# Sliding attention taken in visits of four steps instead of two, its turned weights kept in six places, two of the projection's PSUM banks given up to it

## The chip, the cores and the metric

One NeuronCore of one Trainium2 chip runs the whole program in one launch. The metric is the device time of that launch in microseconds (us), lower is better. TensorE is called PE below (PEld is its weight load), VectorE DVE, ScalarE ACT, GpSimd POOL, and SyncE SP; SP only issues DMAs.

## The reference, cut to what matters

The program computes two transformer blocks and a final norm over 512 tokens of width 1024. Only one part of the second block is touched: its input projection, the sliding-window attention that is computed while that projection runs, and the first product behind them.

```python
z = h @ w_in + b_in                     # 512 x 1024 @ 1024 x 5376 -> 42 tiles of 128 columns
glu_val, glu_gate, q, k, v, g_conv, g_attn = split(z)
q, k = rope(q), rope(k)                 # 16 query heads, 2 key/value heads, head size 64
# blocks of 128 queries see their own and the previous block of 128 keys
s = where(mask, einsum(q, k) * 64 ** -0.5, -1e30)
m = maximum(max(s), sink)
p = exp(s - m) / (sum(exp(s - m)) + exp(sink - m))
attn_out = (p @ v) @ w_attn_o           # 512 x 1024 @ 1024 x 1024
conv_out = conformer_conv(glu_val, glu_gate, ...)   # 31 taps over time, then a layer norm, then a product
```

## The kernel before, in words

Everything is written out by hand: each engine has one instruction stream, and semaphores (`wait_ge`, `then_inc`) tie them together. An engine does its instructions strictly in that order, so one wait holds up all that stands behind it.

**Big products.** Each float32 matrix is split into a high part (rounded, `wh`, `hh`) and a low part (what the rounding left, `wl`, `hl`). `three` (L1383, L1384, L1385) adds three matmuls of 128x128 by 128x512 into a PSUM bank. Eight such triples (index `k`) make one output tile; one triple is called a chunk below. Weights come in slots of 1 MB, each good for two tiles. A slot goes through four hands: SP loads it to `raw[:, b, :]` (`load`, L493, or `load_raw_after`, L550), ACT rounds it to `wh` (`high`, L736), DVE subtracts to get `wl` (`weight_low`, L2059, which raises `w_lo`), and PE uses it. `b` is the slot's number modulo 2, so there are two places for each. Eight slots of the projection (`SPLIT0` and on) were split earlier and come ready from DRAM into `w2` without passing through `raw`; the last slot of the projection (number 69, tiles 40 and 41) and the slots of the next product, "ao", (numbers 70 to 73) go through `raw` again. Slot 70 is the first block of ao, and uses `raw[:, 0, :]`.

**The projection, "in2".** 42 tiles, numbered `t`. Each is written to the bank `IN2_BANKS[t]`; three banks are used in turn from tile 6 on. ACT empties the bank (`in2_out`, L1145, raises `ev_in2`), and PE waits for `ev_in2` of tile `t - 3` before it begins tile `t`.

**Sliding attention.** 32 steps: 8 pairs of heads (`p`) by 4 blocks of queries (`i`). Both heads of a pair are done in one step (`e`). The first block of a pair has 128 key columns, the others 256. A step `n` goes through

- `scores` (PE, L1716): queries times keys, into banks 3 and 4, a half bank for each of two steps
- `masked` (DVE, L2461): scaling, mask and maximum, into `spr[:, n % 2]`
- `exps` and `scaled` (ACT, L1093 to L1105): the softmax
- `turn` (PE, L1727): the weights are transposed into bank 5
- `turned_weights` (ACT, L1114): bank 5 is copied to `spt[:, n % 2]`, in `sqb`
- `values` (PE, L1740): the values times these, into bank 6 or 7
- `heads_out` (ACT, L1121 and L1127), once in four steps, and `y_low` (DVE, L2469, raises `at_l`): the pair's result, split in high and low part for ao.

The steps are spread over tiles 22 to 41 in 35 **beats**. `beat_place` puts beat `n` before chunk `n * 160 // 35` of these tiles, so one comes after every four or five chunks. At a beat PE leaves the projection, does its attention work (a **visit**), and goes back. At an even beat `n` the visit holds `scores` of steps `n` and `n + 1`, `values` of steps `n - 4` and `n - 3`, and `turn` of step `n - 2`; at an odd beat only the `turn`. DVE and ACT have beats of their own in the same order. Between them DVE does the 31 taps of the convolution (`taps`, L2400), 256 instructions of about the same size that fill its time.

**Behind the projection.** ao begins when `w_lo` says that slot 70 is complete. Its first tile takes in piece `k` only when `at_l` has reached `k + 1`, so its last piece waits for `y_low(7)`. ao's fourth and sixth tiles hold the two means of the layer norm (`mean_of_parts`, L1390), for which DVE must have finished the taps and the sums.

## Time and profile before

| | us |
|---|---|
| median of 3 runs (2585.38 to 2585.94) | 2585.47 |
| profiled execution, its own time | 2584.94 |
| its span in the trace | 2583.1 |
| PE busy in the span | 2571.9 |
| DVE, ACT, POOL busy | 1638.5, 1061.1, 426.9 |
| stage of the beats (first `scores` to the last `values`) | 731.3 to 884.6 |

The trace counts from the start of the span. PE's busy time is the union of its matmuls, whose ends are modelled, so a busy PE can still be held back by what stands between two matmuls; the distance from the start of one matmul to the start of the next shows it. In steady work of the projection that distance is 0.227 us.

### The profile page before, as it was taken

The page shows a single profiled execution, that of the slowest core. Times are in us where ns is not written, and L with a number is a line of the kernel's source. Part 1 is how long each engine was busy: PE and PEld are TensorE (multiplying, and loading weights), DVE is VectorE, ACT ScalarE, POOL GpSimd, SP SyncE. Part 2 cuts the span into 40 slices and gives each one's busy share as a digit, 9 for nine tenths or more (in the row PEclk, how much of TensorE's full clock was granted, in tenths as well). Part 3 has the DMA queues.
Part 4 walks back from the last instruction along what each step waited for, and adds up shares of the span by engine and source line. Part 5 has one row for each costly group of instructions (what it writes and reads, how often), then busy time and mean ns, then how long its engine had stood idle before and what let it go on. Part 6 is the DMA issues. An engine that isn't in the chain of part 4 may idle for free.

```text
span 2583.1 us, 33615 instructions
## 1 busy us (share of the span) xinstructions
PE 2571.9 (100%) x12592; PEld 2114.2 (82%) x12592; DVE 1638.5 (63%) x2450; ACT 1061.1 (41%) x1408; POOL 426.9 (17%) x188
## 2 busy tenths in 40 slices
PE   9999999999999999999999999999999999999999
PEld 7778888888877788888888888888888888888887
DVE  6777322304999986689997999999244444444444
ACT  6765433215367753232223555555322222222223
POOL 0002555542022014434443000000000000000000
PEclk9999999999999999999999999999999999999999
DMA  5112664222234222323333455655676655555553
GB/s 190 66 50 82 260 244 179 102 98 98 102 115 163 98 96 100 114 90 146 146 146 147 173 189 191 241 204 187 244 224 207 201 192 191 191 192 190 191 190 126
DMA packets 143324, 410.58 MB, mean 159 GB/s; under 512 B 25552, under 2 KB 91344, under 8 KB 111376
## 3 DMA queue, kind: packets, MB, share of 16 engines
q1 hardware_dynamic: 138400, 353.53, 39.8%
q10 hardware_dynamic: 2016, 34.87, 3.4%
q0 software_dynamic: 2832, 21.24, 2.4%
q8 instruction: 39, 0.64, 0.1%
q14 instruction: 37, 0.30, 0.0%
HBM read 319.16 MB, written 85.98 MB: 157 GB/s over the span
## 4 chain that ended last, share of the span: by engine, by line
PE 98%; ACT 1%; DVE 1%; issue 0%; DMA 0%; SPq 0%; ACTq 0%; DVEq 0%
PE ps L1383 31%; PE ps L1385 30%; PE ps L1384 30%; PE ps L1962 2%; PE ps L1912 1%; PE ps L1716 1%; PE ps L1727 1%; PE ps L1740 1%; PE ps L1598 0%; PE ps L1625 0%; PE ps L1609 0%; DMA raw<-in_w_slots 0%; DVE z L2400 0%; ACT w L736 0%; PE ps L1528 0%
## 5 line engine op out<-in xcount | busy, mean ns | idle before, releaser
L1383 PE MATMUL ps<-hh,w 128*128 128x512 f32 x1968 | 775.3, 394 | 2.3 <-DVE w L2065 2.3
L1385 PE MATMUL ps<-hh,w 128*128 128x512 f32 x1968 | 766.9, 390 | 0.0
L1384 PE MATMUL ps<-hl,w 128*128 128x512 f32 x1968 | 765.8, 389 | 0.0
L736 ACT ACTIVATE w<-raw 128x2048 fp32r<-128x2048 f32 x207 | 395.7, 1912 | 739.9 <-PE ps L1385 739.8
L2694 DVE TENSOR_TENSOR w<-raw,w 128x2048 fp32r<-128x2048 f32 x101 | 231.3, 2290 | 419.4 <-ACT w L736 419.4
L1383 PEld LDWEIGHTS ps<-hh,w 128*128 128x128 f32 x1968 | 369.5, 188 | 86.5 <-issue 7.4
L1385 PEld LDWEIGHTS ps<-hh,w 128*128 128x128 f32 x1968 | 369.4, 188 | 78.4
L1384 PEld LDWEIGHTS ps<-hl,w 128*128 128x128 f32 x1968 | 369.8, 188 | 74.1
L1383 PE MATMUL ps<-w,gah 128*128 128x512 f32 x1024 | 398.3, 389 | 0.0
L1384 PE MATMUL ps<-w,gah 128*128 128x512 f32 x1024 | 398.3, 389 | 0.0
L1385 PE MATMUL ps<-w,gal 128*128 128x512 f32 x1024 | 398.3, 389 | 0.0
L635 POOL TENSOR_TENSOR w<-raw,w 128x2048 fp32r<-128x2048 f32 x50 | 230.5, 4611 | 567.1 <-ACT w L736 567.1
L1385 PEld LDWEIGHTS ps<-w,gal 128*128 128x128 f32 x1024 | 192.3, 188 | 39.9
L1384 PEld LDWEIGHTS ps<-w,gah 128*128 128x128 f32 x1024 | 192.3, 188 | 39.9
L1383 PEld LDWEIGHTS ps<-w,gah 128*128 128x128 f32 x1024 | 192.3, 188 | 39.8
L723 POOL TENSOR_TENSOR pf<-xT,final_rows 128x512 f32<-128x512 f32 x4 | 5.2, 1300 | 1171.0 <-DVE xT L2769 1171.0
L2400 DVE SCALAR_TENSOR_TENSOR z<-z,vec 128x511 f32<-128x511 f32 (+14 forms) x240 | 160.4, 730 | 0.0
L715 POOL TENSOR_TENSOR w<-raw,w 128x2048 fp32r<-128x2048 f32 x27 | 127.1, 4706 | 182.1 <-ACT w L736 182.1
L1272 ACT ACTIVATE ast<-ps 128x512 f32<-128x512 f32 x64 | 38.2, 599 | 239.2 <-PE ps L1385 239.2
L1317 ACT ACTIVATE stage<-ps 128x512 f32<-128x512 f32 x128 | 124.0, 1133 | 0.0
L1307 ACT ACTIVATE ast<-ps 128x512 f32<-128x512 f32 x64 | 38.3, 598 | 194.3 <-PE ps L1385 194.3
L2708 DVE TENSOR_TENSOR same<-iota_t,slot_t 128x1024 f16<-128x1024 f16 x64 | 78.5, 1226 | 43.3 <-PE ps L1962 33.3
(320 smaller groups left out, 3092.6 us busy)
## 6 DMA issues: line engine op xcount, KB each, us to landing
raw<-in_w_slots SPq DMA_DIRECT2D x208, 1024.0 KB, 4.8
a_spill<-ast SPq DMA_DIRECT2D x64, 512.0 KB, 4.7
gate_table<-stage ACTq DMA_DIRECT2D x8, 4096.0 KB, 12.1
at<-a_spill SPq DMA_DIRECT2D x64, 512.0 KB, 5.9
tt<-gate_table SPq DMA_DIRECT2D x64, 512.0 KB, 7.0
w<-split_weights POOLq DMA_DIRECT2D x8, 2048.0 KB, 8.2
split_raw<-in_w_slots SPq DMA_DIRECT2D x8, 1024.0 KB, 6.8
split_weights<-hidl SPq DMA_DIRECT2D x8, 1024.0 KB, 3.8
```

What stands on the lines that cost most here:

```text
L635: pool.tensor_tensor(wl[:, b, :], raw[:, b, :], wh[:, b, :].bitcast(F32), ALU.subtract).then_inc(sem("w_lo"), 1)
L715: pool.tensor_tensor(wl[:, b, :], raw[:, b, :], wh[:, b, :].bitcast(F32), ALU.subtract).then_inc(sem("uv_lo"), 1)
L736: act.activation(wh[:, b, :], raw[:, b, :], ACT.Copy).then_inc(sem("w_hi"), 1)
L1307: act.activation(ast[:, 2 * (i % 2) + j, :], ps[:, 4 + 2 * (i % 2) + j, :], ACT.Gelu).then_inc(sem("a_ev"), 1)
L1317: act.activation(stage[:, q % 2, :, c:c + 4].rearrange("p e c -> p c e"), ps[:, 2 * j + a, :].rearrange("p (c e) -> p c e", c=4), ACT.Copy ...
L1383: nc.tensor.matmul(bank, whi, xhi, start=start, stop=False, skip_group_check=reopened)
L1384: nc.tensor.matmul(bank, whi, xlo, start=False, stop=False, skip_group_check=reopened)
L1385: return nc.tensor.matmul(bank, wlo, xhi, start=False, stop=stop, skip_group_check=reopened)
L1962: last = nc.tensor.matmul(ps[:, 2 * r + t // 4, NKEYS * (t % 4):NKEYS * (t % 4) + NKEYS], oh[r][:, 0, t, :], oh[r][:, part, t, :], start=( ...
L2400: dve.scalar_tensor_tensor(acc[:, back:S], u[:, 0:S - back], w, acc[:, back:S], ALU.mult, ALU.add).then_inc(sem("cv2_y" if m == TAPS else ...
L2694: dve.tensor_tensor(wl[:, b, :], raw[:, b, :], wh[:, b, :].bitcast(F32), ALU.subtract).then_inc(sem("uv_lo"), 1)
L2708: dve.tensor_tensor(same[:, :, :], iota_rows, slots(0), ALU.is_equal).then_inc(sem("oh_part"), 1)
```

## The change

1. PE's visits: `scores` and `values` are done for four steps at once, every fourth beat. `scores` of steps `n` to `n + 3` at beats 0, 4, ..., 28; `values` of steps `n - 8` to `n - 5` at beats 8, 12, ..., 32, and of the last four steps at beat 34. `turn` stays at each beat.
2. The scores need four half-bank pairs: banks 3 and 4, and banks 1 and 7. Bank 1 is taken from the projection, whose tiles from 21 on use banks 0 and 2 in turn, and PE waits for `ev_in2` of tile `t - 2`. `values` uses bank 6, and for the last pair bank 7.
3. The turned weights have six places: two in `sqb`, four in `raw[:, 0, :]`, which is idle while slots come ready from DRAM.
4. Therefore SP loads slot 70 only when `values` of all 32 steps is done (`sw_o`). ACT's `high` for it moves from tile 39 to tile 40 of its order; DVE's `weight_low` stays at tile 40, with five taps put before it.
5. ACT empties a tile's bank before the beats of the next tile instead of behind them; `heads_out` and `y_low` come two beats later; ao's first tiles wait for other semaphores, as their banks are other ones.

```diff
+TWO_BANKS = BEAT_TILE0 - 1
+IN2_BANKS = [1, 2, 0, 3, 4, 5] + [(t + 1) % 3 for t in range(6, TWO_BANKS)] + [t % 2 * 2 for t in range(TWO_BANKS, Z2_TILES)]
+SCORE_BANKS = ((3, 4), (1, 7))
+VALUE_BANKS = [6] * (SWA_PAIRS - 1) + [7]
+TURNED_SLOTS = 6
...
+        def spt(n):
+            r = n % TURNED_SLOTS
+            rows = sqb[:, r, :] if r < 2 else raw[:, 0, (r - 2) * S:(r - 1) * S]
+            return rows.rearrange("p (e n) -> p e n", e=2)
...
             for g in (after, after + 1):
                 sp.wait_ge(sem("w_used"), g - 1)
+                if g % 2 == 0:
+                    sp.wait_ge(sem("sw_o"), SWA_STEPS)
                 load_raw_after(g)
...
                 act.wait_ge(sem("sw_t"), n + 1)
-                if n >= 2:
-                    act.wait_ge(sem("sw_o"), n - 1)
+                if n == 0:
+                    act.wait_ge(sem("w_lo"), SPLIT0 + 2)
+                if n >= TURNED_SLOTS:
+                    act.wait_ge(sem("sw_o"), n - TURNED_SLOTS + 1)
...
-                if n >= 7 and (n - 7) % NT == 0:
-                    heads_out((n - 7) // NT)
+                if n >= 9 and (n - 9) % NT == 0:
+                    heads_out((n - 9) // NT)
...
             for t in range(Z2_TILES + 1):
+                if t > TWO_BANKS:
+                    in2_out(t - 1)
                 for n in beats_in(t):
                     beat(n)
...
-                if t >= 4:
+                if 4 <= t <= TWO_BANKS:
                     in2_out(t - 1)
...
+                late = t in (Z2_TILES - 3, Z2_TILES - 2)
+                if late and t % 2 == 0:
+                    high(g0 + t // 2 + 1, (g0 + t // 2 + 1) % 2)
...
-                if n % 2 == 0:
+                if i == 0:
                     pe.wait_ge(sem("sw_q"), p + 1)
-                    if n:
-                        pe.wait_ge(sem("sw_m"), 2 * n)
+                if n % 2 == 0 and n >= NT:
+                    pe.wait_ge(sem("sw_m"), 2 * n - NT)
...
             def beat(n):
-                if n % 2 == 0:
-                    for m in (n, n + 1):
-                        if m < SWA_STEPS:
-                            scores(m)
-                    for m in (n - 4, n - 3):
-                        if 0 <= m < SWA_STEPS:
-                            values(m)
+                if n % NT == 0 and n < SWA_STEPS:
+                    for m in range(n, n + NT):
+                        scores(m)
+                if n % NT == 0 and n >= 2 * NT:
+                    for m in range(n - 2 * NT, n - NT):
+                        values(m)
+                if n == BEATS - 1:
+                    for m in range(SWA_STEPS - NT, SWA_STEPS):
+                        values(m)
                 if 0 <= n - 2 < SWA_STEPS:
                     turn(n - 2)
...
-                    pe.wait_ge(sem("ev_in2"), t - 2)
+                    pe.wait_ge(sem("ev_in2"), t - 2 if t < TWO_BANKS else t - 1)
...
-                if n < 3:
-                    pe.wait_ge(sem("ev_in2"), Z2_TILES - 2 + n)
+                if n in (1, 2):
+                    pe.wait_ge(sem("ev_in2"), Z2_TILES)
                 elif n < 5:
                     pe.wait_ge(sem("sw_m"), 2 * SWA_STEPS)
...
-                if n >= 9 and (n - 9) % NT == 0:
-                    y_low((n - 9) // NT)
+                if n >= 11 and (n - 11) % NT == 0:
+                    y_low((n - 11) // NT)
...
                         dve.sem_inc(sem("w_lo"), SPLIT_SLOTS)
+                    if t == Z2_TILES - 2:
+                        taps(5)
                     weight_low(g0 + t // 2 + 1)
...
-            taps(12)
+            y_low(SWA_PAIRS - 2)
+            taps(7)
             y_low(SWA_PAIRS - 1)
             weight_low(g0 + 1)
             taps(KD * conv_steps)
```

How the change moves instructions, at three places. First PE at beat 8, where a pair of heads begins (`scores` write `ps` from `kdup`, `values` read `sqb` or `raw`, `turn` reads `tmp_all`). Before, the whole visit:

```order
L1716 MATMUL ps<-kdup,z 128x128 [waits sw_m,sw_q]
L1716 MATMUL ps<-kdup,z 128x128
L1716 MATMUL ps<-kdup,z 128x256 x2
L1740 MATMUL ps<-sqb,z 64x128 [waits sw_pt]
L1740 MATMUL ps<-sqb,z 64x128
L1740 MATMUL ps<-sqb,z 64x128 [waits sw_pt]
L1740 MATMUL ps<-sqb,z 64x128 x3
L1727 MATMUL ps<-cst,tmp_all 128x128 [waits sw_pt,sw_p]
L1727 MATMUL ps<-cst,tmp_all 128x128 x3
```

and with the change, from the third step's `scores` on (the first two stand ahead of it as before):

```order
L1735 MATMUL ps<-kdup,z 128x256 [waits sw_m]
L1735 MATMUL ps<-kdup,z 128x256 x3
L1761 MATMUL ps<-sqb,z 64x128 [waits sw_pt]
L1761 MATMUL ps<-sqb,z 64x128
L1761 MATMUL ps<-sqb,z 64x128 [waits sw_pt]
L1761 MATMUL ps<-sqb,z 64x128 x3
L1761 MATMUL ps<-raw,z 64x128 [waits sw_pt]
L1761 MATMUL ps<-raw,z 64x128 x3
L1761 MATMUL ps<-raw,z 64x128 [waits sw_pt]
L1761 MATMUL ps<-raw,z 64x128 x3
L1746 MATMUL ps<-cst,tmp_all 128x128 [waits sw_pt,sw_p]
```

Four steps' `scores` and `values` stand where two were; beats 6 and 10 keep only their `turn`.

Second ACT at the end of the projection, around `turned_weights` of steps 30 and 31 (L1114; L1145 is `in2_out`, L736 `high`, L1121 and L1127 `heads_out`). Before:

```order
L1145 ACTIVATE z<-ps,vec 128x512 [waits half_mm]
L736 ACTIVATE w<-raw 128x2048 [waits w_used,w_raw0]
L1114 ACTIVATE sqb<-ps 128x512 [waits sw_o,sw_t] x2
L1145 ACTIVATE z<-ps,vec 128x512 [waits w_used]
L1145 ACTIVATE z<-ps,vec 128x512 [waits half_mm]
L736 ACTIVATE w<-raw 128x2048 [waits w_used,w_raw1]
L1145 ACTIVATE z<-ps,vec 128x512 [waits w_used]
L1121 ACTIVATE z<-ps 128x512 [waits sw_o]
L1127 ACTIVATE csinr<-z 128x512 [waits sw_q,sw_y]
```

and with the change (the same helpers are L1128, L1159, L748, L1135 and L1141):

```order
L1128 ACTIVATE sqb<-ps 128x512 [waits sw_o,sw_t] x2
L1135 ACTIVATE z<-ps 128x512 [waits sw_o]
L1141 ACTIVATE csinr<-z 128x512 [waits sw_q,sw_y]
L748 ACTIVATE w<-raw 128x2048 [waits w_used,w_raw0]
L1159 ACTIVATE z<-ps,vec 128x512 [waits half_mm]
L748 ACTIVATE w<-raw 128x2048 [waits w_used,w_raw1]
L1159 ACTIVATE z<-ps,vec 128x512 [waits w_used]
L1135 ACTIVATE z<-ps 128x512 [waits sw_o]
L1141 ACTIVATE csinr<-z 128x512 [waits sw_q,sw_y]
```

`high` of slot 70 (`w_raw0`) stood before `turned_weights` of steps 30 and 31, and now stands behind them and behind a `heads_out`.

Third DVE, behind `weight_low` of slot 70, from the last of three taps to `weight_low` of slot 71, with the change (L2423 is one tap, L2492 `y_low`, L2082 `weight_low`):

```order
L2423 SCALAR_TENSOR_TENSOR z<-z,vec 128x490 [waits cv2_1]
L2492 TENSOR_TENSOR z2r<-z,csinr 128x512 [waits at_h]
L2423 SCALAR_TENSOR_TENSOR z<-z,vec 128x489 [waits cv2_0]
L2423 SCALAR_TENSOR_TENSOR z<-z,vec 128x489 [waits cv2_1]
L2423 SCALAR_TENSOR_TENSOR z<-z,vec 128x488 [waits cv2_0]
L2423 SCALAR_TENSOR_TENSOR z<-z,vec 128x488 [waits cv2_1]
L2423 SCALAR_TENSOR_TENSOR z<-z,vec 128x487 [waits cv2_0]
L2423 SCALAR_TENSOR_TENSOR z<-z,vec 128x487 [waits cv2_1]
L2423 SCALAR_TENSOR_TENSOR z<-z,vec 128x486 [waits cv2_0]
L2492 TENSOR_TENSOR z2r<-z,csinr 128x512 [waits at_h]
L2082 TENSOR_TENSOR w<-raw,w 128x2048 [waits w_hi]
```

Before, both low parts stood apart by fifteen taps and one `y_low`; with the change it is ten taps and two `y_low`, and five taps have gone ahead of slot 70's.

## Rows read from the trace of the kernel before

**Rows 1.** Page of the profile: busy time, share of the span, instructions.

```profile
PE 2571.9 (100%) x12592; PEld 2114.2 (82%) x12592; DVE 1638.5 (63%) x2450; ACT 1061.1 (41%) x1408; POOL 426.9 (17%) x188
```

**Rows 2.** Waits of 731 to 884 us: total, times, longest.

```profile
DVE tmp_all L2461 <- PE ps L1727: 10.4, 11, 1.6
...
PE ps L1727 <- ACT sqb L1114: 0.6, 1, 0.6
```

**Rows 3.** Timeline of PE, visits of beats 4 and 6: start, length, merged.

```profile
746.58 0.93 PE L1716 MATMUL ps<-kdup,z 64*128 64x128 f32 x8
747.44 0.93 PE L1740 MATMUL ps<-sqb,z 128*64 128x128 f32 x12
748.29 0.66 PE L1727 MATMUL ps<-cst,tmp_all 128*128 128x128 f32 x4
...
755.18 0.39 PE L1385 MATMUL ps<-hh,w 128*128 128x512 f32 x1
755.50 1.13 PE L1716 MATMUL ps<-kdup,z 64*128 64x256 f32 x8
756.57 1.15 PE L1740 MATMUL ps<-sqb,z 128*64 128x128 f32 x16
757.64 0.44 PE L1727 MATMUL ps<-cst,tmp_all 128*128 128x128 f32 x2
...
758.15 0.39 PE L1384 MATMUL ps<-hl,w 128*128 128x512 f32 x1
```

**Rows 4.** Timeline of PE, visit of beat 3, a turn alone.

```profile
742.37 0.40 PE L1385 MATMUL ps<-hh,w 128*128 128x512 f32 x1
742.60 0.60 PE L1727 MATMUL ps<-cst,tmp_all 128*128 128x128 f32 x4
...
743.28 0.39 PE L1384 MATMUL ps<-hl,w 128*128 128x512 f32 x1
```

**Rows 5.** Timeline of PE, turns of beats 29 and 33.

```profile
860.96 0.39 PE L1385 MATMUL ps<-hh,w 128*128 128x512 f32 x1
861.47 0.63 PE L1727 MATMUL ps<-cst,tmp_all 128*128 128x128 f32 x4
...
878.48 0.39 PE L1385 MATMUL ps<-hh,w 128*128 128x512 f32 x1
879.46 0.63 PE L1727 MATMUL ps<-cst,tmp_all 128*128 128x128 f32 x4 [0.59 <-ACT sqb L1114]
```

**Rows 6.** Timeline of PE: last values, first ao matmul, ao's eighth piece.

```profile
883.45 1.15 PE L1740 MATMUL ps<-sqb,z 128*64 128x128 f32 x16
...
888.06 0.39 PE L1383 MATMUL ps<-z2r,w 128*128 128x512 f32 x1
...
892.82 0.42 PE L1383 MATMUL ps<-csinr,w 128*128 128x512 f32 x1
```

**Rows 7.** Timeline of ACT: high part of slot 70.

```profile
876.93 1.90 ACT L736 ACTIVATE w<-raw 128x2048 fp32r<-128x2048 f32 x1
```

**Rows 8.** Timeline of DVE: fifteen taps, last y_low, low part of slot 71.

```profile
881.30 9.68 DVE L2400 SCALAR_TENSOR_TENSOR z<-z,vec 128x493 f32<-128x493 f32 x15
891.99 0.69 DVE L2469 TENSOR_TENSOR z2r<-z,csinr 128x512 fp32r<-128x512 f32 x1 [1.01 <-ACT csinr L1127]
892.60 2.29 DVE L2059 TENSOR_TENSOR w<-raw,w 128x2048 fp32r<-128x2048 f32 x1
```

**Rows 9.** Source L550: the two loads behind the ready slots.

```profile
DMA to landing us min/median/max: 4.7/4.8/4.8
```

**Rows 10.** Timeline of DVE, then PE: layer norm's second mean.

```profile
920.38 0.69 DVE L2045 TENSOR_TENSOR sqr<-z,sqr 128x512 fp32r<-128x512 f32 x1
...
921.26 0.39 PE L1390 MATMUL ps<-sqr,cst_r 128*128 128x512 f32 x1
```

**Rows 11.** Stretches at the end: PE, PEld, DVE, ACT, POOL; PEclk, DMA, GB/s.

```profile
2576.00:2578.00 2.00, 1.18 (x6) 0.64 (x4) 1.33 (x4) 1.87 (x6) 1.29 (x1) 1.00 0.41 153
...
2579.00:2580.00 1.00, 0.00 (x0) 0.00 (x0) 0.74 (x1) 0.81 (x2) 0.00 (x0) 0.62 0.42 160
```

More of the change, by code:

```diff
@@ L213 @@
 RAW_TILES = 6
-IN2_BANKS = [1, 2, 0, 3, 4, 5] + [(t + 1) % 3 for t in range(6, Z2_TILES)]
+TWO_BANKS = BEAT_TILE0 - 1
[3 more added lines that the diff above has]
+TURNED_SLOTS = 6
 def rolled(eng, n, unroll, body):
@@ L1111, in turned_weights @@
                 act.wait_ge(sem("sw_t"), n + 1)
[L1112 to L1114 removed]
+                if n == 0:
+                    act.wait_ge(sem("w_lo"), SPLIT0 + 2)
+                if n >= TURNED_SLOTS:
+                    act.wait_ge(sem("sw_o"), n - TURNED_SLOTS + 1)
+                act.activation(spt(n).rearrange("p e (b n) -> p e b n", b=2)[:, :, b:, :],
                                ps[:, 5, :].rearrange("p (e b n) -> p e b n", e=2, b=2)[:, :, b:, :], ACT.Copy
@@ L1120, in heads_out @@
                 act.wait_ge(sem("sw_o"), NT * p + NT)
-                act.activation(u_tile(Q2 + p), ps[:, 6 + p % 2, :], ACT.Copy).then_inc(sem("sw_y"), 1)
+                act.activation(u_tile(Q2 + p), ps[:, VALUE_BANKS[p], :], ACT.Copy).then_inc(sem("sw_y"), 1)
                 act.wait_ge(sem("sw_y"), p + 1)
@@ L1174, in _ @@
                         in2_out(a)
-                if t < Z2_TILES and t % 2 and t != RAW_TILES - 1 and not is_split(g0 + t // 2 + 2):
+                late = t in (Z2_TILES - 3, Z2_TILES - 2)
+                if late and t % 2 == 0:
+                    high(g0 + t // 2 + 1, (g0 + t // 2 + 1) % 2)
+                if t < Z2_TILES and t % 2 and not late and t != RAW_TILES - 1 and not is_split(g0 + t // 2 + 2):
                     if g0 + t // 2 + 2 == SPLIT0 + SPLIT_SLOTS:
@@ L1709, in scores @@
                 kv, r = p // PAIRS_PER_KV, n % 2 * 2 * P
-                if n % 2 == 0:
+                if i == 0:
                     pe.wait_ge(sem("sw_q"), p + 1)
-                    if n:
-                        pe.wait_ge(sem("sw_m"), 2 * n)
+                if n % 2 == 0 and n >= NT:
+                    pe.wait_ge(sem("sw_m"), 2 * n - NT)
                 for e in range(2):
                     h = slice(HD * e, HD * e + HD)
-                    last = nc.tensor.matmul(ps[:, 3 + e, r + c:r + 2 * P], z2[h, Q2 + p, i * P:i * P + P],
+                    last = nc.tensor.matmul(ps[:, SCORE_BANKS[n // 2 % 2][e], r + c:r + 2 * P], z2[h, Q2 + p, i * P:i * P + P],
                                             kdup[h, kv, (i - 1) * P + c:(i + 1) * P], start=True, stop=True)
@@ L1735, in values @@
                 pe.wait_ge(sem("sw_pt"), n + 1)
-                if i == 0 and p > 1:
-                    pe.wait_ge(sem("sw_y"), p - 1)
+                if i == 0 and p == SWA_PAIRS - 1:
+                    pe.wait_ge(sem("sw_m"), 2 * SWA_STEPS)
+                elif i == 0 and p:
+                    pe.wait_ge(sem("sw_y"), p)
                 for e in range(2):
                     for k in range(c, 2 * P, P):
-                        last = nc.tensor.matmul(ps[HD * e:HD * e + HD, 6 + p % 2, i * P:i * P + P],
+                        last = nc.tensor.matmul(ps[HD * e:HD * e + HD, VALUE_BANKS[p], i * P:i * P + P],
                                                 vn(i - 1 + k // P)[:, HD * kv:HD * kv + HD],
-                                                spt[:, n % 2, e, k:k + P], start=(k == c), stop=(k == P))
+                                                spt(n)[:, e, k:k + P], start=(k == c), stop=(k == P))
                 last.then_inc(sem("sw_o"), 1)
             def beat(n):
-                if n % 2 == 0:
-                    for m in (n, n + 1):
-                        if m < SWA_STEPS:
-                            scores(m)
-                    for m in (n - 4, n - 3):
-                        if 0 <= m < SWA_STEPS:
-                            values(m)
+                if n % NT == 0 and n < SWA_STEPS:
[7 more added lines that the diff above has]
+                        values(m)
                 if 0 <= n - 2 < SWA_STEPS:
@@ L2460, in masked @@
                 for e in range(2):
-                    dve.tensor_tensor_reduce(spr[:, n % 2, e, c:2 * P], ps[:, 3 + e, r + c:r + 2 * P], msk[:, c:], -SCALE,
+                    dve.tensor_tensor_reduce(spr[:, n % 2, e, c:2 * P], ps[:, SCORE_BANKS[n // 2 % 2][e], r + c:r + 2 * P], msk[:, c:], -SCALE,
                                              nsink[:, 2 * p + e:2 * p + e + 1], ALU.add, ALU.min,
```

2 lines of the change are left out of this document (removed).

## The prediction

> **What bounds the kernel now.** I read the page first. PE is busy for 2571.9 us of a span of 2583.1 [rows 1], so the other engines matter only where PE waits for them, and every hundredth of a microsecond between two of its matmuls counts. Next I asked for the waits of the stage that the change touches, 731 to 884 us. PE hardly waits there: 0.6 us in all is booked, on `turned_weights`. DVE on the other hand waits 10.4 us for PE's turns [rows 2], so it has that much to spare in the stage. What PE loses there is not waiting but switching, and that is seen only in the starts of its matmuls, so the third view was PE's timeline.
>
> A steady product of the projection starts 0.227 us after the one before it. The seven pieces between ao's first matmul and its eighth piece (21 matmuls) take 892.82 - 888.06 = 4.76 us, which is 0.227 each and 0.68 for a chunk [rows 6]. A visit is what its neighbours are apart beyond that. A turn alone costs 743.28 - 742.37 - 2 x 0.227 = 0.46 us for its four matmuls, 0.114 each [rows 4]. The visit of beat 6 costs 758.15 - 755.18 - 2 x 0.227 = 2.52 us [rows 3].
>
> How much of the 2.52 is work? I compare it with beat 4, which has the same groups with less in them [rows 3].
> - `scores` to `values`: 1.07 us for eight matmuls of 256 columns, 0.86 where four of the eight have 128. Halving four saves 0.21, so four of 256 are 0.42 and eight 0.84. Left: 0.23 for the switch.
> - `values` to `turn`: 1.07 us for sixteen matmuls, 0.85 for twelve. Four are 0.22, sixteen 0.88. Left: 0.19.
> - Entry: 755.50 - 755.18 - 0.227 = 0.09 us.
> - Two turns and the way back: 758.15 - 0.227 - 757.64 = 0.28 us against 0.23 at the price of rows 4. Left: 0.05.
>
> So a visit with both `scores` and `values` costs 0.56 us over its work, and a turn alone nothing.
>
> **The change, part by part.**
>
> *Fewer visits.* Before, `scores` and `values` meet at beats 4, 6, ..., 30: 14 visits. With the change they meet at 8, 12, ..., 28: six. The visits with only one of them are two and two in both. All matmuls stay. Saved: 8 x 0.56 = **4.5 us**.
>
> *Late turns.* At beats 29 and 33 the turn starts 861.47 - 860.96 = 0.51 and 879.46 - 878.48 = 0.98 us after the product before it [rows 5], 0.28 and 0.75 more than the steady 0.227. Both follow a `high` on ACT, 1.90 us long [rows 7], which stands before the `turned_weights` that the turn needs. The change puts the second `high` behind both copies, and a `heads_out` no longer stands before the first. Saved: **1.0 us**.
>
> *New waits in the stage.* None of them is in the trace, so I bound them. (a) The third `scores` of a visit waits for `masked` of the step before the visit. DVE has 10.4 us to spare over the stage [rows 2], and PE becomes at most 5.5 us faster, so on the whole DVE keeps up; but the visits at which only a turn is left come about 2 us sooner after the last one. (b) With two banks PE needs tile `t - 2` emptied; ACT does that before the next beats. (c) ACT's copies have up to 2 us less before a turn at every second even beat. The least is nothing. For the most I take that half of each of the seven later `scores` visits waits as long as the first late turn, 0.28 us, and that two tiles and two turns wait as much: 7.5 x 0.28 = 2.1 us. I take 0.5, near the lower end, because of the 10.4 us.
>
> Together PE comes to the end of `values` 4.5 + 1.0 - 0.5 = **5.0 us** earlier.
>
> *The load of slot 70.* Here the time is given back. Before, the last `values` ends at 883.45 + 1.15 = 884.60 [rows 6]; now at 879.6. Only then may SP issue the load. Five chunks of the projection are left to PE, and before it went over to ao without a gap at 888.06 [rows 6]; now it would at 883.1. But the load lands after 4.8 us [rows 9], at 884.4; ACT rounds for 1.90 [rows 7], to 886.3; DVE subtracts for 2.29 [rows 8], to **888.6**. PE stands idle for 5.5 us, and ao begins 0.5 us later than before. The next load, of slot 71, is issued right behind, and PE needs it only at ao's third tile, 10.9 us later: covered.
>
> *What stands behind the low part on DVE.* DVE comes to `weight_low` of slot 70 long before 886.3: between `masked(31)` and it there are 14 taps of 9.68 / 15 = 0.645 us and one `y_low` [rows 8]. So it waits too, and the order holds everything else up. Behind it come three taps, `y_low(6)`, seven taps and `y_low(7)`: 10 x 0.645 + 2 x 0.61 = 7.7 us (0.61 is 892.60 - 891.99 [rows 8]), to **896.2**. PE takes in the eighth piece of ao's first tile only then. Its first seven pieces need 4.76 us from 888.6, to 893.4, so it waits again, 2.8 us. Before, that piece began at 892.82 [rows 6]: PE is **3.4 us late**.
>
> *After that.* Behind `y_low(7)` stand the low part of slot 71 and the nine last taps, as before, so DVE stays about 3.6 us late (892.6 to 896.2), as PE does. The second mean of the layer norm has little room: DVE's instruction for it ends at 920.38 + 0.69 = 921.07, PE uses it at 921.26 [rows 10]. 0.2 us of DVE's extra lateness fits in. Nothing further on makes up time, as PE is the bound there: +3.4 us stays to the end.
>
> *The clock.* In the trace PE's clock is full (1.00, the level of 2.4 GHz) while it works; its last matmuls lie in the stretch 2576 to 2578 with 1.18 us of work, and in 2579 to 2580 the mean is 0.62, on its way to the half level of 1.2 GHz [rows 11]. So some 2 us of standing still were enough there, and 5.5 us may well be here. At half speed the seven pieces before the wait on `y_low(7)` take at most 9.5 instead of 4.76 us and would end at 898.1, 1.9 us behind 896.2. If the clock comes back halfway, they end at 895.7 and the wait hides it all. I take nothing for it, and 1.9 us as the upper bound. The Trainium skill (TensorE: Matmul & The Clock Gate, section "What's actually happening") says that the throttled state is the default and that activity releases it, so it speaks against a change that makes PE stand still; by it ao would begin cold and the sum would go from +3.4 towards +5.3.
>
> **Sum.** -4.5 - 1.0 + 0.5 up to the last `values`, +5.5 for the block, +2.8 for `y_low(7)`, 0.1 for rounding: +3.4 us. The profiled execution took 2584.94 us, 0.5 less than the median of 2585.47; the sum applied to the median gives **2588.9 us**. A measurement of this kernel can tell about 0.2%, 5.2 us, from no change, so this counts as the same, on the slow side.
>
> **The rivals.**
> - *DVE or ACT sets the pace of the beats, or the cold clock outlasts the wait (slower by over 0.2%).* One place, PE's share of the time between beat 4 and ao's eighth piece. For it: the thin rooms of (a) to (c), and rows 11. Against: the 10.4 us of rows 2, and that a later piece waits anyway. Taken as one mechanism, the small waits at their upper bound: +2.1 - 0.5 = 1.6 more, so +5.0 us, 2590.5; it decides from 2.3 us of waits on, which is where 0.2% begins. With the clock's bound on top it would be +6.9, 2592.4. Chance 0.14.
> - *The taps do not matter (same, nearer to before).* If `y_low(7)` were not what PE waits for, ao would only begin 0.5 us late: 2586.0. Against it stands the order of DVE, in which nothing lets `y_low(7)` pass. Chance 0.08.
> - *Switches cost less in the longer visits or the load is quicker (same).* Had every switch its price and the small waits none, and the load its shortest 4.7 us [rows 9], the sum is +2.8, 2588.3. Chance part of the forecast.
> - *Faster by over 0.2%.* This needs the whole saving of 5.5 us and no wait for slot 70. The load cannot begin before the last `values`, and 4.8 + 1.9 + 2.29 us stand against five chunks of 0.68. Or the saving would have to be much larger than rows 3 show. Chance 0.03. That the change doesn't do what it says is not open: the order shows it.
>
> **How the numbers follow.** Forecast (2588.9, from 2587.9 to 2590.4) 0.75, slower rival 0.14, taps rival 0.08, faster 0.03. The range leaves out most of the faster case and the far end of the slower one: 2585.8 to 2591.8. Faster 0.03, same 0.83, slower 0.14.
>
> **What would show it.** In the trace of the changed kernel: eight visits with `scores`, six of them with `values`, each with 0.56 us over its work; turns of beats 29 and 33 without delay; the last `values` ending near 879.6; a wait of PE of about 5.5 us for `w` from DVE before the first ao matmul, near 888.6; a second one of 1 to 3 us at the eighth piece, for `y_low`, until 896.2; PEclk below 1.00 between. Wrong would be: no second wait (then the taps rival), a first wait much shorter than 5 us, or waits of over 2 us in all at `scores`.

## The result, and the profile after

| | before | changed |
|---|---|---|
| median of 22 runs each | 2585.18 us | 2589.56 us |
| range of the runs | 2584.28 to 2586.23 | 2588.52 to 2592.20 |
| profiled execution | 2584.94 us, span 2583.1 | 2588.69 us, span 2586.9 |

The ratio of after to before is 1.0017, with a 95% interval of 1.0012 to 1.0023: 4.4 us slower. That is clear of zero, but less than the 0.2% (5.2 us) below which two times count as the same here. The forecast was 2588.9 us (2585.8 to 2591.8).

The page of the changed kernel has PE busy as before [rows 1]:

```profile
PE 2570.0 (99%) x12592; PEld 2116.0 (82%) x12592; DVE 1638.4 (63%) x2450; ACT 1060.8 (41%) x1408; POOL 429.8 (17%) x188
```

The difference shows in the waits. First the waits of all engines from 725 to 960 us (total, times, longest), two of them:

```profile
DVE w L2082 <- ACT w L748: 8.6, 2, 8.1
ACT w L748 <- DMA raw<-in_w_slots: 8.3, 1, 8.3
```

Then the same stretch, PE alone:

```profile
PE ps L1402 <- DVE w L2082: 5.6, 1, 5.6
PE ps L1402 <- DVE z2r L2492: 0.7, 1, 0.7
PE ps L1746 <- ACT raw L1128: 0.4, 1, 0.4
```

Before, PE had one wait of 0.6 us up to 884 us [rows 2]. Now a chain of three stands still at once: ACT for the load of slot 70, DVE for ACT's high part, PE for DVE's low part.

**The visits** got what was promised. Timeline of PE (start, length, operation), the visit of beat 12:

```profile
778.70 0.39 PE L1404 MATMUL ps<-hh,w 128*128 128x512 f32 x1
779.02 1.79 PE L1735 MATMUL ps<-kdup,z 64*128 64x128 f32 x16
780.74 0.93 PE L1761 MATMUL ps<-raw,z 128*64 128x128 f32 x12
781.45 1.09 PE L1761 MATMUL ps<-sqb,z 128*64 128x128 f32 x16
782.47 0.66 PE L1746 MATMUL ps<-cst,tmp_all 128*128 128x128 f32 x4
782.88 0.47 PE L1402 MATMUL ps<-hh,w 128*128 128x512 f32 x1
783.20 0.39 PE L1403 MATMUL ps<-hl,w 128*128 128x512 f32 x1
```

By the prediction's reading, `scores` to `values` are 1.72 us for twelve matmuls of 0.105 and four of half that, 1.47: 0.25 for the switch. `values` to `turn` are 1.73 for 28 x 0.055 = 1.54: 0.19. With 0.09 at the entry and 0.04 on the way back that is 0.57 for a visit of four steps, as it was 0.56 for one of two [rows 3].

One late turn is new, at beat 19. Timeline of PE, then what ACT did before its copy:

```profile
810.60 0.39 PE L1404 MATMUL ps<-hh,w 128*128 128x512 f32 x1
811.38 0.63 PE L1746 MATMUL ps<-cst,tmp_all 128*128 128x128 f32 x4 [0.40 <-ACT raw L1128]
```

```profile
809.14 0.58 ACT L1135 ACTIVATE z<-ps 128x512 f32<-128x512 f32 x1
809.75 0.64 ACT L1141 ACTIVATE z2r<-z 128x512 fp32r<-128x512 f32 x1
810.29 0.67 ACT L1159 ACTIVATE z<-ps,vec 128x512 f32<-128x512 f32 x1
810.86 0.37 ACT L1128 ACTIVATE raw<-ps 128x256 f32<-128x256 f32 x1
```

`heads_out` (two instructions) and `in2_out` stand before `turned_weights`; the turn is 811.38 - 810.60 - 0.227 = 0.55 us late.

**The block.** Timeline of PE from the last `values` to ao's eighth piece:

```profile
878.37 1.09 PE L1761 MATMUL ps<-sqb,z 128*64 128x128 f32 x16
...
882.70 0.39 PE L1404 MATMUL ps<-hh,w 128*128 128x512 f32 x1
888.67 0.80 PE L1402 MATMUL ps<-z2r,w 128*128 128x512 f32 x1 [5.58 <-DVE w L2082]
...
892.25 0.54 PE L1404 MATMUL ps<-z2r,w 128*128 128x512 f32 x1
892.63 0.39 PE L1402 MATMUL ps<-z2r,w 128*128 128x512 f32 x1
...
895.15 0.39 PE L1404 MATMUL ps<-csinr,w 128*128 128x512 f32 x1
896.25 0.50 PE L1402 MATMUL ps<-csinr,w 128*128 128x512 f32 x1 [0.71 <-DVE z2r L2492]
```

and the three engines ahead of it, SP, ACT and DVE in turn:

```profile
879.57 0.33 SPq L560 DMA_DIRECT2D raw<-in_w_slots  x1
```

```profile
884.38 1.91 ACT L748 ACTIVATE w<-raw 128x2048 fp32r<-128x2048 f32 x1 [8.28 <-DMA raw<-in_w_slots]
```

```profile
886.32 2.29 DVE L2082 TENSOR_TENSOR w<-raw,w 128x2048 fp32r<-128x2048 f32 x1 [8.13 <-ACT w L748]
888.53 2.00 DVE L2423 SCALAR_TENSOR_TENSOR z<-z,vec 128x491 f32<-128x491 f32 x3
890.45 0.69 DVE L2492 TENSOR_TENSOR z2r<-z,csinr 128x512 fp32r<-128x512 f32 x1
891.05 4.55 DVE L2423 SCALAR_TENSOR_TENSOR z<-z,vec 128x489 f32<-128x489 f32 x7
895.52 0.68 DVE L2492 TENSOR_TENSOR z2r<-z,csinr 128x512 fp32r<-128x512 f32 x1
```

The last `values` end at 879.46 and free the place; the load is issued 0.1 us later, and ao starts at 888.67, 5.58 us of it waiting. ao's first matmuls then start 0.427 us apart instead of 0.227. The seven pieces last until 895.38 instead of 893.4, and the wait for `y_low(7)` is 0.87 us (896.25 - 895.15 - 0.227), not 2.8. The clock behind that, in stretches of 2 us (columns as in [rows 11]); it is at 0.50 from 886 on and comes back between 892 and 894:

```profile
884.00:886.00 2.00, 0.00 (x0) 0.00 (x0) 0.00 (x0) 1.62 (x1) 0.00 (x0) 0.93 0.99 422
886.00:888.00 2.00, 0.00 (x0) 0.00 (x0) 1.68 (x1) 2.00 (x3) 0.00 (x0) 0.50 0.09 37
...
892.00:894.00 2.00, 2.00 (x9) 1.62 (x8) 2.00 (x4) 2.00 (x5) 0.00 (x0) 0.86 0.43 180
```

**Behind the block** nothing makes up time. Timeline of DVE, then PE, at the layer norm's second mean, 3.5 us later than in [rows 10] and again with 0.2 us between them:

```profile
923.91 0.69 DVE L2068 TENSOR_TENSOR sqr<-z,sqr 128x512 fp32r<-128x512 f32 x1
```

```profile
924.80 0.40 PE L1409 MATMUL ps<-sqr,cst_r 128*128 128x512 f32 x1
```

Two executions differ by up to 3 us before the stage begins, because of waits at the very start of the program. So I measure within an execution, from the start of the first `scores` on, against the kernel before (731.29, 892.82 and 921.26: 161.5 us to the eighth piece, 190.0 to the second mean). "Trace" below is that difference; "runs" is the difference of medians to the runs of the kernel before that were made beside them.

| kernel | median us | runs | trace: eighth piece | second mean |
|---|---|---|---|---|
| changed | 2589.56 | +4.4 | +4.0 | +4.1 |
| e1 places elsewhere | 2581.79 | -3.5 | -4.2 | -4.1 |
| e10 two steps, two value banks | 2584.83 | -0.1 | -0.8 | -0.7 |
| e8 one step | 2592.51 | +7.5 | +6.8 | +6.8 |
| e2 two steps, one value bank | 2589.38 | +4.1 | +4.3 | +4.3 |
| e4 two banks alone | 2585.35 | +0.1 | 0.0 | 0.0 |
| e3 late load alone | 2592.68 | +7.4 | +7.1 | +7.2 |
| e5 y_low(7) first | 2589.15 | +4.2 | +4.1 | +4.2 |
| e6 PE kept busy | 2591.12 | +6.0 | +4.1 | +5.8 |
| e7 both | 2589.81 | +4.7 | +1.4 | +4.0 |
| e11 taps in the wait | 2588.14 | +2.9 | +2.9 | +2.9 |
| e12 taps in the wait, PE busy | 2586.83 | +1.6 | +1.4 | +1.4 |
| e9 small waits | 2582.06 | -2.9 | -3.6 | -3.3 |

The medians of before beside them were 2584.97 to 2585.26; the intervals of the ratios are about 0.1% (2.6 us) to either side, so below a microsecond the trace says more than the runs. One of e4's twelve executions, at 2682.42 us, fell into a slower state of the chip and is left out of its median.

### The profile page after: what moved, and what is told of

It reads as the page before. It is cut to its first block, busy times and chain, and to the rows that moved or that the text cites. A ratio compares the mean times of both kernels' runs of the same rounds, so it can differ in the third digit from the quotient of the medians.

```text
span 2586.9 us, 33606 instructions
## 1 busy us (share of the span) xinstructions
PE 2570.0 (99%) x12592; PEld 2116.0 (82%) x12592; DVE 1638.4 (63%) x2450; ACT 1060.8 (41%) x1408; POOL 429.8 (17%) x188
## 4 chain that ended last, share of the span: by engine, by line
PE 97%; DVE 1%; ACT 1%; DMA 0%; issue 0%; SPq 0%; DVEq 0%; ACTq 0%
PE ps L1402 30%; PE ps L1404 30%; PE ps L1403 30%; PE ps L1985 2%; DVE z L2423 1%; PE ps L1935 1%; PE ps L1761 0%; PE ps L1735 0%; PE ps L1617 0%; PE ps L1746 0%; PE ps L1644 0%; DMA raw<-in_w_slots 0%; PE ps L1628 0%; ACT w L748 0%; DVE tmp_all L2484 0%
## 5 line engine op out<-in xcount | busy, mean ns | idle before, releaser
L748 ACT ACTIVATE w<-raw 128x2048 fp32r<-128x2048 f32 x207 | 395.7, 1912 | 747.4 <-PE ps L1404 738.9
L2423 DVE SCALAR_TENSOR_TENSOR z<-z,vec 128x511 f32<-128x511 f32 (+14 forms) x240 | 161.2, 737 | 0.0
```

The costliest lines, as they stand in the source:

```text
L748: act.activation(wh[:, b, :], raw[:, b, :], ACT.Copy).then_inc(sem("w_hi"), 1)
L2423: dve.scalar_tensor_tensor(acc[:, back:S], u[:, 0:S - back], w, acc[:, back:S], ALU.mult, ALU.add).then_inc(sem("cv2_y" if m == TAPS else ...
```

## The experiments

### Is it the late load that gives the saving back?

e1 takes from the changed kernel what makes the load late: the four places in `raw`.

```diff
-            rows = sqb[:, r, :] if r < 2 else raw[:, 0, (r - 2) * S:(r - 1) * S]
+            last = n == SWA_STEPS - 5
+            rows = (sqb[:, r, :] if r < 2 else kdup[:, 0, :] if last
+                    else (z2[:, ORDER2[40], :], z2[:, ORDER2[39], :], z2[:, ORDER2[41], :], lnb[:, 1, :])[r - 2])
...
-                if g % 2 == 0:
-                    sp.wait_ge(sem("sw_o"), SWA_STEPS)
```

> From the changed kernel: the four places for turned weights that lie in raw go to z2 tiles and buffers that are free then (one goes to kdup), and the load of slot 70 no longer waits for the last values. Order of ACT and DVE as in the changed kernel. My theory (the time is given back because the load of slot 70 starts only after the last values): the first ao matmul starts near 883.1 without a wait for w, and ao's eighth piece near 888, so PE is about 5 us earlier than before there; DVE's order of taps and the layer-norm means allow nearly all of it: 2580.2 to 2581.5 us, 8 to 9 us under the changed kernel. Rival (DVE's order of taps before y_low is what binds, the load only seems to): the eighth piece still waits for y_low until some 892 or later, 2585 us or more. Rival (the switches cost no time, the visits save nothing): about 2585 us, as before, with the last values at their old time.

Measured: 2581.79 us, 7.8 under the changed kernel and 3.5 under before (ratio 0.9987, interval 0.9978 to 0.9996). ao starts at 883.64 without a wait; the eighth piece waits 0.34 us for `y_low(7)`:

```profile
888.75 0.50 PE L1402 MATMUL ps<-csinr,w 128*128 128x512 f32 x1 [0.18 <-DVE z2r L2492]
```

e3 does the opposite: the kernel before, with nothing but the late load and the order of ACT and DVE that goes with it.

```diff
+                if g % 2 == 0:
+                    sp.wait_ge(sem("sw_o"), SWA_STEPS)
                 load_raw_after(g)
...
-                if t < Z2_TILES and t % 2 and t != RAW_TILES - 1 and not is_split(g0 + t // 2 + 2):
+                late = t in (Z2_TILES - 3, Z2_TILES - 2)
+                if late and t % 2 == 0:
+                    high(g0 + t // 2 + 1, (g0 + t // 2 + 1) % 2)
+                if t < Z2_TILES and t % 2 and not late and t != RAW_TILES - 1 and not is_split(g0 + t // 2 + 2):
...
+                    if t == Z2_TILES - 2:
+                        taps(5)
                     weight_low(g0 + t // 2 + 1)
...
-            taps(12)
+            taps(7)
```

> From the kernel before: only the load of slot 70 is held until after the last values, as in the changed kernel, with its high part behind the copies and DVE's taps placed as there; visits of two steps stay. My theory: the last values at 883.9 to 884.6, load 4.8, high 1.9, low 2.3, so ao starts at 893 to 893.6; then y_low(7) holds the eighth piece until about 901, where before it was at 892.8: +7 to +8.5 us over before, 2592.3 to 2593.8. Rival (the late load is hidden and the changed kernel loses in its beats): within 2 us of before. Rival (only the block of w counts, the taps before y_low(7) are hidden): +5.5 us, 2590.7.

Measured: +7.4 us. ao started at 892.67 after a wait of 5.4, the eighth piece at 899.66. So the late load costs 7.4 us on the old visits and 7.8 on the new ones (7.2 and 8.2 by the trace). Of the 1.0 us between the last two, 0.75 is the turn of beat 33, which comes on time in e3 and is late in the kernel before. So the cost hardly depends on the visits. The rival that it is hidden falls by the runs; the one with 5.5 us falls by the trace, for the interval of the runs reaches down to it.

### What does a visit cost, apart from its work?

e2 is e1 with visits of two steps again. `heads_out` and `y_low` go back by two beats as before; these lines are left out below.

```diff
...
-                if n % NT == 0 and n < SWA_STEPS:
-                    for m in range(n, n + NT):
-                        scores(m)
-                if n % NT == 0 and n >= 2 * NT:
-                    for m in range(n - 2 * NT, n - NT):
-                        values(m)
...
+                if n % 2 == 0:
+                    for m in (n, n + 1):
+                        if m < SWA_STEPS:
+                            scores(m)
+                    for m in (n - 4, n - 3):
+                        if 0 <= m < SWA_STEPS:
+                            values(m)
...
```

> As the run with the places elsewhere, but with visits of two steps again (14 visits with both groups instead of six). My theory: the eight switches come back at 0.56 us each, so 4.5 us (4 to 5) over the run with the places elsewhere, close to the kernel before (2584.5 to 2586). Rival (what the places and the two banks save is the waits, not the switches): under 1.5 us over the run with the places elsewhere.

Measured: 7.6 us over e1, too much for both. The waits of PE name the mistake, which is the experiment's own:

```profile
PE ps L1760 <- ACT z L1134: 5.0, 6, 1.3
```

With one bank for the values of all pairs but the last, `values` of a new pair wait for `heads_out` to empty it; with visits of two steps these come two beats after the last ones into that bank, and ACT reaches `heads_out` only at the end of the beat between. In the changed kernel the next ones come four beats later. e10 repeats it with before's banks and the waits that go with them (left out below).

```diff
-SCORE_BANKS = ((3, 4), (1, 7))
-VALUE_BANKS = [6] * (SWA_PAIRS - 1) + [7]
+SCORE_BANKS = ((3, 4), (3, 4))
+VALUE_BANKS = [6 + p % 2 for p in range(SWA_PAIRS)]
...
```

> The run with visits of two steps was mixed up with a wait: with one bank for the values, PE waited six times, 5.0 us in all, for ACT to empty it. Here the visits of two steps have the kernel before's banks (scores in 3 and 4, values in 6 and 7 by turns) and everything else as in the run with the places elsewhere. My theory: no waits on heads_out; the visits between 731 and 884 cost 46.1 us over the steady pace, 3.8 more than with four steps (eight switches of 0.56 less the one late turn of 0.57 there), so 3.2 to 3.8 over the run with the places elsewhere: 2584.3 to 2585.6 us. Rival (switches cost less than 0.56 each and waits explain the saving): under 2 us over it, below 2583.8.

Measured: 2584.83 us, 3.0 over e1, and 3.4 by the trace. No wait is booked on `heads_out`. Summed over all visits, PE spends 46.4 us beyond the steady pace, against 42.3 in e1. One late turn is in each, and makes its whole visit 0.31 us longer here and 0.57 there, so eight visits cost 46.4 - 42.3 + 0.57 - 0.31 = 4.4 us, 0.54 each.

e8 goes the other way, from e10 to a visit at every beat; DVE then waits for the `scores` of one step instead of two.

```diff
-                if n % 2 == 0 and n:
+                if n:
                     pe.wait_ge(sem("sw_m"), 2 * n)
...
-                if n % 2 == 0:
-                    for m in (n, n + 1):
-                        if m < SWA_STEPS:
-                            scores(m)
-                    for m in (n - 4, n - 3):
-                        if 0 <= m < SWA_STEPS:
-                            values(m)
+                if n < SWA_STEPS:
+                    scores(n)
+                if 0 <= n - 3 < SWA_STEPS:
+                    values(n - 3)
...
```

> As the run with two steps and two value banks, but visits of one step at every beat (29 visits with scores and values instead of 14). My theory: 15 more switches at 0.56, and one more visit each with scores or values alone at about 0.3: +8.4 to +9.2 us over that run, if scores then don't wait for masked. Rival (the price of a visit grows with its groups' length, not with their number): under 2 us over it. Rival (the switch is a fixed price only because it covers waits): cost per visit clearly other than 0.56.

Measured: +7.7 us over e10, a little under what was expected. The visits take 53.5 us beyond the steady pace against e10's 46.4 (46.1 without its late turn): 7.4 more, for 15 more visits with both groups and two more with one of them. No wait of PE is booked. One of them on PE's timeline:

```profile
810.13 0.39 PE L1403 MATMUL ps<-hh,w 128*128 128x512 f32 x1
810.45 0.70 PE L1734 MATMUL ps<-kdup,z 64*128 64x256 f32 x4
811.09 0.67 PE L1758 MATMUL ps<-z 128*64 128x128 f32 x8
811.68 0.66 PE L1745 MATMUL ps<-cst,tmp_all 128*128 128x128 f32 x4
812.09 0.47 PE L1401 MATMUL ps<-hh,w 128*128 128x512 f32 x1
812.41 0.39 PE L1402 MATMUL ps<-hl,w 128*128 128x512 f32 x1
```

0.09 at the entry, 0.64 - 4 x 0.105 = 0.22, 0.59 - 8 x 0.055 = 0.15, and 0.04 back: 0.50. Then 29 such visits instead of 14 at 0.56 are 6.7 us, and 0.7 is left for the two visits with one group. The price belongs to the visit and hardly grows with its length (0.50, 0.56 and 0.57 for one, two and four steps). It stands where the shape of the tile changes, from 128*128 to 64*128, to 128*64, and back; a turn, which is 128*128 like the projection, costs nothing [rows 4], though PE waits for semaphores before it as well. So the waiting instructions as such are not the price. The Trainium skill has a rule for this (TensorEngine Tiling (Array Packing), section "Key Properties"): "Changing tiling mode (not just tile) drains the TensorE". These rows agree.

e4 tests the other part of the visits, the two banks, on the kernel before.

```diff
-IN2_BANKS = [1, 2, 0, 3, 4, 5] + [(t + 1) % 3 for t in range(6, Z2_TILES)]
+TWO_BANKS = BEAT_TILE0 - 1
+IN2_BANKS = [1, 2, 0, 3, 4, 5] + [(t + 1) % 3 for t in range(6, TWO_BANKS)] + [t % 2 * 2 for t in range(TWO_BANKS, Z2_TILES)]
```

> From the kernel before: only the projection's tiles go to two banks, and ACT empties a tile before the beats of the next. My theory: PE finds a bank free at every tile, and nothing changes: within 0.5 us of before. Rival (two banks cost a wait of PE at each tile): 13 tiles with 0.1 to 0.3 us each, +1.5 to +4 us.

Measured: +0.1 us by the runs, 0.0 by the trace. Two banks are free of charge.

### Behind the block: order, clock, or both?

e5 takes the seven taps out from ahead of `y_low(7)`.

```diff
             y_low(SWA_PAIRS - 2)
-            taps(7)
             y_low(SWA_PAIRS - 1)
+            taps(7)
             weight_low(g0 + 1)
```

> From the changed kernel: y_low(7) stands right behind y_low(6) on DVE, the seven taps between them go behind it. The prediction's theory (what holds the eighth piece is the taps, 2.8 us of wait that fall away): 2586.8 us. My theory after the trace of the changed kernel (the pieces before run at the half clock until 895.2, which used up most of that wait; and DVE is late at the second mean all the same): 0 to 0.9 us faster, 2588.7 to 2589.5, with the eighth piece starting near 895.4 and a new wait at the layer norm's second mean.

Measured: 2589.15 us, 0.2 to 0.4 faster, which these runs can't tell from nothing. In its profile the eighth piece follows the seventh without a wait, but the seven pieces took 7.5 us (891.49 to 898.98) instead of 6.7, because the half clock reached farther into ao in this execution. The matmuls 0.427 us apart go on for 5.3 us behind ao's start (to 896.77), where it was 3.6 in the changed kernel. The stretch of 2 us that begins 4.5 us behind ao's start, columns as in [rows 11]:

```profile
896.00:898.00 2.00, 2.00 (x8) 1.62 (x7) 2.00 (x4) 2.00 (x5) 0.00 (x0) 0.73 0.00 0
```

So the trace has no gain at either point (+4.1, +4.2), and the early eighth piece that I expected (near 895.4) did not come. This execution was the slowest of e5's eleven (2591.46 us), mostly since its first `scores` came 2.6 us later than in the changed kernel's; so what e5 is worth where the clock comes back sooner, no trace shows.

e6 keeps PE at work through its wait. It adds 24 products that nobody reads.

```diff
+            pe.wait_ge(sem("sw_m"), 2 * SWA_STEPS)
+            for n in range(24):
+                nc.tensor.matmul(ps[:, 3, :], mean_r, hh[:, n % KD, :], start=True, stop=True)
             for n in range(KD):
                 b, half = (g0 + n // 2) % 2, n % 2
```

> From the changed kernel: 24 added products of 512 columns into a bank that nobody reads stand on PE before its wait for the low part of slot 70, so that PE works through the wait; nothing else changes. My theory: the granted clock stays at 1.00 over 884 to 894, ao's first seven pieces take 4.8 us instead of 6.3 and end near 893.5, but then the eighth piece waits for y_low(7) until 896.2: the wait grows from 0.7 to about 2.6 us and the time stays, within 0.5 us of the changed kernel. Rival (the cold clock is what costs): 1.5 us faster.

Measured: 2591.12 us, 1.6 slower; neither theory had that. The first half went as I expected: the granted clock is 1.00 until 896, the seventh piece ends at 893.4, the eighth waits 2.5 us. Then it comes. Timeline of PE, and stretches of 2 us:

```profile
896.09 0.50 PE L1402 MATMUL ps<-csinr,w 128*128 128x512 f32 x1 [2.51 <-DVE z2r L2495]
896.43 0.44 PE L1403 MATMUL ps<-z2r,w 128*128 128x512 f32 x1
896.67 0.63 PE L1404 MATMUL ps<-csinr,w 128*128 128x512 f32 x1
...
899.65 0.59 PE L1402 MATMUL ps<-z2r,w 128*128 128x512 f32 x1
900.08 0.40 PE L1403 MATMUL ps<-z2r,w 128*128 128x512 f32 x1
```

```profile
894.00:896.00 2.00, 0.00 (x0) 0.00 (x0) 2.00 (x5) 1.90 (x4) 0.00 (x0) 1.00 0.00 0
896.00:898.00 2.00, 1.91 (x6) 1.53 (x7) 2.00 (x2) 0.00 (x0) 0.00 (x0) 0.66 0.00 0
898.00:900.00 2.00, 2.00 (x6) 1.60 (x5) 2.00 (x4) 0.00 (x0) 0.00 (x0) 0.50 0.40 57
```

The standstill of 2.5 us brings the clock down to the half level (1.2 GHz) after all, and now no wait lies behind it: eight gaps of 0.427 instead of 0.227 are 1.6 us, and so much is added between the eighth piece and the second mean (+4.1 to +5.8). In the changed kernel the clock's loss was hidden in the wait for `y_low(7)`; the added products took it out of the hiding place and put it on the path.

The median depends on how often that happens. The eleven executions took 2588.63 to 2591.74 us. The three shortest (to 2589.50) had a mean granted clock of 1.000 over the whole program, the eight longer ones (from 2590.18) 0.999. So the clock probably stayed up in those three, and then the added products cost nothing; only one of the eleven has a trace, so this is not shown.

e7 joins the two edits.

> From the changed kernel: both of the last two edits, the added products and y_low(7) before the seven taps. My theory: the eighth piece starts near 893.5, 2.7 us earlier, but the layer norm's second mean needs DVE, whose work before it has not become less and which has 0.2 us of room there, so PE waits there for most of what was won: 0 to 1 us faster than the changed kernel. Rival (both waits of the block count in full): 2.7 us faster, 2586.9.

Measured: 2589.81 us, 0.2 over the changed kernel (+4.7 against +4.4). The eighth piece comes 2.7 us earlier (+1.4 against +4.0), and all of it is gone again by the second mean (+4.0):

```profile
PE ps L1409 <- DVE sqr L2071: 2.3, 2, 1.9
```

That is the layer norm's means waiting for `sum_low` on DVE. So the lateness does not sit in PE's waits; it sits in DVE, which stood still for 8.1 us before slot 70's low part and has the same work behind it as ever. Hence e11: twelve more taps into that standstill, in addition to e5's order. The twelve are e5's seven behind `y_low(7)` and five of the nine behind slot 71's low part.

```diff
                     if t == Z2_TILES - 2:
-                        taps(5)
+                        taps(17)
                     weight_low(g0 + t // 2 + 1)
...
             y_low(SWA_PAIRS - 2)
-            taps(7)
             y_low(SWA_PAIRS - 1)
             weight_low(g0 + 1)
```

> From the changed kernel: twelve more taps stand on DVE ahead of the low part of slot 70, inside the 8.1 us in which it waits there (12 x 0.645 = 7.7 us), and the seven between y_low(6) and y_low(7) are gone from behind it. My theory (DVE's order behind the block is what hands the lateness on, and the clock is the second part): ao still starts near 888.6 and its first seven pieces run cold until 895.2, but the eighth follows at once, and DVE comes early to both means of the layer norm: 0.9 to 1.2 us faster than the changed kernel, 2588.3 to 2588.7, with no other wait of PE behind ao's start. Rival (the clock does not matter): 3.4 us faster, 2586.2. Rival (DVE's order does not matter): no change, 2589.6.

e12 is e11 with e6's products.

> As the run before it in this call, with the 24 added products on PE ahead of its wait for slot 70. My theory: the clock stays at 1.00, no piece waits, the means do not wait: what is left of the late load is the 0.5 to 0.9 us by which ao starts late. 2.0 to 3.2 us faster than the changed kernel, 2586.4 to 2587.6, and 1.5 to 2.2 us faster than without the added products (where these cost 1.5 us as long as the eighth piece still waited). Rival (the added products only move the cold stretch to a later wait): no faster than without them.

Measured: 2588.14 and 2586.83 us (+2.9 and +1.6 over before). DVE's standstill in e11 shrinks to 0.45 us:

```profile
870.45 16.11 DVE L2423 SCALAR_TENSOR_TENSOR z<-z,vec 128x497 f32<-128x497 f32 x25
887.01 2.29 DVE L2082 TENSOR_TENSOR w<-raw,w 128x2048 fp32r<-128x2048 f32 x1 [0.45 <-ACT w L748]
```

Both carry their difference from the eighth piece to the second mean unchanged (+2.9, +2.9 and +1.4, +1.4), with no wait of PE behind ao's start. Only now is the cold clock worth something: 1.3 us between the two, 1.5 by the trace. Added products that cost 1.6 us with DVE late save 1.3 with DVE on time.

### A version that beats both

e1 is one. e9 was to take its last small waits away: `y_low(7)` first, `heads_out(7)` before a `high`, the other `heads_out` a beat later.

```diff
-                if n >= 9 and (n - 9) % NT == 0:
-                    heads_out((n - 9) // NT)
+                if n >= 10 and (n - 10) % NT == 0:
+                    heads_out((n - 10) // NT)
...
+                if t == Z2_TILES - 1:
+                    heads_out(SWA_PAIRS - 1)
```

> From the run with the places elsewhere: y_low(7) stands right behind y_low(6) on DVE with the seven taps behind it, heads_out(7) on ACT stands before the high part of the projection's last but one slot, and every other heads_out one beat later. My theory: the late turn at beat 19 (0.57) and the wait at ao's eighth piece (0.34) go, but DVE's work up to the layer norm's second mean stays what it is and has 0.2 us of room there, so only 0 to 0.4 us is gained: 2581.4 to 2581.8 us. Rival (PE's waits count in full): 0.9 us, 2580.9. Rival (the order brings a new late turn or DVE waits for heads_out): up to 1 us slower.

Measured: 2.9 under before, where e1 was 3.5 under; the runs don't tell the two apart. The late turn of beat 19 and the wait at the eighth piece are gone, and in their place stands a wait at the `scores` of beat 28 (and `values` of beat 20 that start 0.5 us late):

```profile
PE ps L1736 <- issue: 1.0, 1, 1.0
```

The profile names no releaser for it, so its cause stays open.

Pushing ACT's work around moves the small waits and doesn't remove them. e1 stays the best, with the gain of the visits and none of the load's cost.

## Why the prediction was right

Point by point, from the first `scores` on (the prediction's 888.6 is 157.3 us behind them, its 896.2 is 164.9):

- *Fewer visits, -4.5.* Measured 8 x 0.54 = 4.4 (e10 against e1), and the visits of four steps cost 0.57 over their work. Right.
- *Late turns, -1.0.* The turns of beats 29 and 33 are on time: 0.28 + 0.75. Right.
- *New waits, +0.5.* One came, 0.55 us at beat 19, through cause (c), ACT. `scores` waited nowhere for `masked`. Right in size, somewhat by luck.
- *End of `values`.* 148.8 us behind the first `scores`, against 153.3 before: 4.5 earlier instead of 5.0. Of the 0.5, 0.1 is the switches and 0.05 the new late turn; the products that follow a visit started a little farther apart (0.3 us over the stage), which the prediction had no term for.
- *Load, high, low.* 879.46 to 888.67 is 9.2 us against 9.0. PE's wait is 5.58, forecast 5.5.
- *`y_low(7)`.* From the start of slot 70's low part to the eighth piece 9.9 us, by the forecast 9.9 as well (886.3 to 896.2). The eighth piece came 4.0 us late within the stage, forecast 3.4; the 0.65 between them are the two items above. The wait itself was 0.87, not 2.8, since the cold clock filled the rest.
- *The clock, 0.* The bounds were 0 and 1.9 us, and the case in which the clock comes back halfway and the wait hides the loss is what happened: the seven pieces ended at 895.4. Even the longer cold stretch of e5 (7.5 us to the eighth piece) would have fitted into the 7.6 us that the changed kernel's eighth piece came behind ao's start, though only just. The Trainium skill (TensorE: Matmul & The Clock Gate, section "What's actually happening") calls the throttled state the default, which activity releases. This trace agrees, for ao began at a granted clock of 0.50; the +5.3 worked out from it did not come, since the wait for DVE covered the loss. e12 against e11 shows what it is worth uncovered: 1.3 us.
- *The means' room, 0.2 us.* Right, and more important than the prediction made it. e7 shows that DVE's lateness would hold PE there even if the eighth piece had come on time. The prediction named the taps before `y_low(7)` as the cause of the second half of the loss. They are one of two places where the same lateness of DVE surfaces; taking only them away (e5, e7) gains nothing that the runs or traces can tell, giving DVE work in its standstill (e11) gains 1.2 to 1.5 us. So +2.8 for `y_low(7)` was right as the lateness of the eighth piece, and only in part as a cause: without that wait the time would have stayed nearly the same (e7).
- *The sum.* +3.4 forecast, +4.1 in the trace at the second mean, +4.4 by the medians. Of the rivals, "the taps do not matter" falls in its number (2586.0), and "faster" needed the load not to wait for the last `values`, which is e1.

Nearly all of what the late load costs (7.8 us between e1 and the changed kernel, 8.2 by the trace) is now accounted for. In microseconds by the medians, and by the trace at the second mean in brackets: 5.1 (5.5) is ao's later start alone (e12 to e1), 1.3 (1.5) the cold clock (e11 to e12), 1.3 (1.3) DVE's standstill (e5 to e11). The intervals of the medians are wider than the two small parts, so these rest on one trace for each kernel. The parts also belong to this order of edits: with DVE late, a clock kept up gained nothing (e6, e7).

## What to carry to other kernels

When a change frees PE time by borrowing a buffer, ask which transfer waits for that buffer and who stands still along its chain: an engine of 63% load that stands still for 8 us in front of a dense stretch is as late as PE itself. Count PE's changes of tile shape: they cost about half a microsecond per visit here, whether it held one step or four. And a filler that keeps the clock up paid here only when no later wait on PE was left (e12), not while one was (e6, e7).

## What the runs showed of the hardware

I had not expected that keeping PE busy could make the kernel slower. After a standstill of 5.6 us (changed kernel) ao's matmuls were 0.427 us apart for 3.6 us (888.67 to 892.25), with the granted clock at 0.50 since 886. After a standstill of only 2.5 us behind full-speed work (e6) they were at the old pace for two matmuls, and then 0.427 apart from 896.67 to 900.08. The wait of 0.87 us at the eighth piece of the changed kernel left the clock at 1.00, and so did the one of 1.9 us at e7's first mean (1.00 from 908 to 912). In e6 the fall of the clock thus came after PE was at work again, where a look at the wait alone would not find it.
